# Third mixer: latents, keys and values copied in another order, transposes of the exponents two heads behind the scores, with a third buffer

## The chip, the core and the metric

The kernel runs on one core of a Trainium2 chip. A core has five engines that run their own instruction queues side by side and meet at semaphores: TensorE (PE in the rows; the loads of its weights are PEld), VectorE (DVE), ScalarE (ACT), GpSimd (POOL) and SyncE (SP), which here only issues DMAs. The metric is the device time of one execution in microseconds (us), and the figure given for a kernel is the median of its runs.

## The reference, cut to what matters

Two residual blocks work on 256 tokens of width 1024. The part that is changed is the last of three mixers, attention with latents:

```python
def mla_mixer(h, positions, w_in, q_norm_g, w_uq, kv_norm_g, w_ukv, w_o):
    q_a, kv_a, k_rope = jnp.split(h @ w_in, [Q_LORA, Q_LORA + KV_LORA], axis=-1)
    q = (rmsnorm_2(q_a, q_norm_g) @ w_uq).reshape(bsz, L, MLA_HEADS, QK_NOPE + QK_ROPE)
    q_nope, q_rope = q[..., :QK_NOPE], q[..., QK_NOPE:]
    kv = (rmsnorm_2(kv_a, kv_norm_g) @ w_ukv).reshape(bsz, L, MLA_HEADS, QK_NOPE + V_DIM)
    k_nope, v = kv[..., :QK_NOPE], kv[..., QK_NOPE:]
    q_rope = apply_rope(q_rope, cos[:, :, None], sin[:, :, None])
    k_rope = apply_rope(k_rope, cos, sin)
    ...
        s = (jnp.einsum("bqhd,bkhd->bhqk", qn, k_nope, preferred_element_type=jnp.float32)
             + jnp.einsum("bqhd,bkd->bhqk", qr, k_rope, preferred_element_type=jnp.float32)) * scale
        s = jnp.where(k_idx[None, :] <= q_idx[:, None], s, -jnp.inf)
        p = jax.nn.softmax(s, axis=-1).astype(v.dtype)
        return jnp.einsum("bhqk,bkhd->bqhd", p, v)
    ...
    return o @ w_o
```

There are 16 heads; the query latents have width 768, the latents of keys and values 256; a head has 64 unrotated and 32 rotated query and key rows and 64 value columns.

## The kernel before

All weights are streamed in blocks of 128x2048 numbers (1 MB). SP loads a block into one of three slots of `raw`. ACT rounds it to `whi` (`act_split`, line 176), DVE takes the residue `raw - whi` to `wlo` (`dve_split`, line 184), and PE multiplies in three passes: high by high, high by low and low by high. So each engine has splits standing in its queue among its other work, and their place in the queue is written out by hand. ACT may split a block once PE has used the block three before it; SP may load once DVE has split the block three before.

A block of the third mixer is numbered from `F0`: four blocks of the input projection, one of keys (`UKV0`, function `uk`), one of values (`uv`), eight of queries (`UQ0`, `uq`), four of the output projection (`OUT0`).

The entry of the mixer runs so. ACT copies each pair of latent tiles out of its bank (line 1785) and squares it (1787). PE sums the squares, ACT takes the root (`root`, 1773), DVE the reciprocal and the scaling by two multiplications per instruction (`scale_latent`, 1879 and 1882; group 0 are the two tiles for keys and values, group 1 the six for queries). ACT rounds a pair of scaled tiles to `xh` (`round_latent`, 1769), DVE takes the residue to `xl` (`rest`, 1870). PE computes keys for all heads into the four banks `ACC` (line 1628), the values into the banks `GATE`, `UP`, `MODP` and `STAT` (line 1646), and the first query block into `GATE` again (line 1670). The key copies of ACT (`m3_kt`, 1797), the value copies of ACT (1803) and of DVE (1908) empty these banks. The rotated part of the key is the same for all heads: `rotate_k` on DVE (lines 1890 to 1893) leaves it in `kr`, and GpSimd copies it 16 times into `m3_kt` (line 1849).

The attention then goes by turns `j`, each with one query block (two heads) and the scores of the two heads `h = 2 (j - 2)` and `h + 1`. A turn has on PE: half of the query block, `attend(h)`, the other half, `attend(h + 1)`, and `swap_q` (1681), which permutes rows for the rotation. For `swap_q` ACT first copies the query block to `m3_qs` (1841). GpSimd and DVE do the rotation: GpSimd multiplies by the cosine (1857), DVE by the sine (`rope_q`, 1917), GpSimd adds (1861). `attend(h)` has the scores into bank `h % 2` (1695, 1696 and the mask, 689), DVE's maxima (1923) and their scaling (1925), ACT's exponents (1811), DVE's reciprocals and weights (1929, 1932), the transposes of the exponents on PE into bank 2 (`turn`, 1705), ACT's copy to `m3_pt` (1818), for two heads the sums over the values into bank 3 (`sums`, 1716), and their split into `m3_o_hi` (ACT, 1828) and `m3_o_lo` (DVE, 1946). The exponents have two buffers, so that those of head `h` wait for the transposes of head `h - 2`. In the last turns the output projection (288) takes the place of the query blocks.

In the rows of the profile the tensors `m3_...` are called `m_...`, all PSUM banks `bank`, and `ident` is `consts`.

## Time and profile before

| | us |
|---|---|
| median of three runs | 1700.56 (1700.59, 1700.56, 1698.80) |
| the profiled execution | 1694.85 |
| its span, first to last instruction | 1693.2 |
| PE busy | 1659.2 (98%) |
| DVE busy | 1201.0 (71%) |
| ACT busy | 809.7 (48%) |
| POOL busy | 85.3 (5%) |
| mean granted TensorE clock | 0.992 of 2.4 GHz |

Busy time on an engine is no more than presence: PE is the engine on which nearly the whole chain of work lies that ended last (87% of it). The timeline lists instructions with start, length and, in brackets, how long the engine had been idle before and what released it. The third mixer fills the time from about 1353 to 1494 us.

### The profile page before, as it was taken

To read this page: it belongs to the slowest core of one execution; us is meant where nothing else is said; L and a number is where in the kernel's file an instruction comes from. 1 tells how busy PE (TensorE), PEld (TensorE's weight loads), DVE (VectorE), ACT (ScalarE), POOL (GpSimd) and SP (SyncE) were. 2 spreads that over 40 slices of the span, in tenths; PEclk is the share of its full clock that TensorE was granted. 3 is DMA by queue.
4 is the path that set the end of the run, shared out by engine and by line. 5 is a ranking of instruction groups with operands and counts; after the bars stand their busy time and mean duration, and the time that the engine had idled before them with its cause. 6 is when DMAs were issued, how large, how long until landed. Compare 5 with 4: busy or idle time off the path is not lost.

```text
span 1693.2 us, 34456 instructions
## 1 busy us (share of the span) xinstructions
PE 1659.2 (98%) x14544; PEld 1623.7 (96%) x14544; DVE 1201.0 (71%) x1303; ACT 809.7 (48%) x874; POOL 85.3 (5%) x110
## 2 busy tenths in 40 slices
PE   9999999999999999999998899999999999999998
PEld 9999999999999999999998899999999987899998
DVE  6888876676788886888867688756544566765444
ACT  5444556644544444444565554345344456554442
POOL 0000000000000000000003000000000003200000
PEclk9999999999999999999999999999999999999999
DMA  8998744344499874988533359653655433345551
GB/s 322 348 339 305 267 176 175 139 159 151 164 350 328 309 266 171 349 311 323 205 135 123 125 208 339 250 196 127 222 199 183 170 144 126 125 148 201 199 188 61
DMA packets 50491, 365.08 MB, mean 216 GB/s; under 512 B 5728, under 2 KB 5856, under 8 KB 6240
## 3 DMA queue, kind: packets, MB, share of 16 engines
q1 hardware_dynamic: 39744, 287.04, 46.2%
q0 software_dynamic: 10368, 75.50, 12.0%
q8 instruction: 74, 1.21, 0.3%
q10 hardware_dynamic: 288, 1.18, 0.2%
q14 instruction: 17, 0.14, 0.0%
HBM read 362.65 MB, written 1.05 MB: 215 GB/s over the span
## 4 chain that ended last, share of the span: by engine, by line
PE 87%; DVE 7%; ACT 3%; issue 1%; DMA 1%; SPq 0%; ACTq 0%; DVEq 0%
PE bank L252 50%; PE bank L288 24%; PE bank L271 3%; PE bank L244 3%; DVE wlo L184 2%; PE bank L361 2%; PE bank L1670 1%; PE bank L373 1%; ACT whi L176 1%; DVE m_p L1435 1%; DVE m_e L1932 0%; DVE x L313 0%; ACT m_e L1811 0%; DMA raw<-stream_in 0%; DVE x L405 0%
## 5 line engine op out<-in xcount | busy, mean ns | idle before, releaser
L184 DVE TENSOR_TENSOR wlo<-raw,whi 128x2048 fp32r<-128x2048 f32 x261 | 598.1, 2294 | 200.7 <-ACT whi L176 200.2
L252 PE MATMUL bank<-xh,whi 128*128 128x256 f32 x2608 | 727.3, 279 | 3.5 <-DVE wlo L184 1.9
L252 PE MATMUL bank<-xl,whi 128*128 128x256 f32 x2608 | 721.7, 277 | 0.0
L252 PE MATMUL bank<-xh,wlo 128*128 128x256 f32 x2608 | 721.4, 277 | 0.0
L176 ACT ACTIVATE whi<-raw 128x2048 fp32r<-128x2048 f32 x261 | 498.2, 1913 | 300.4 <-PE bank L252 177.1
L252 PEld LDWEIGHTS bank<-xh,whi 128*128 128x128 f32 x2608 | 491.1, 188 | 6.1 <-issue 3.2
L252 PEld LDWEIGHTS bank<-xl,whi 128*128 128x128 f32 x2608 | 490.1, 188 | 0.1
L252 PEld LDWEIGHTS bank<-xh,wlo 128*128 128x128 f32 x2608 | 490.0, 188 | 0.0
L288 PE MATMUL bank<-hid_hi,whi 128*128 128x256 f32 x1056 | 291.9, 276 | 0.0
L288 PE MATMUL bank<-hid_lo,whi 128*128 128x256 f32 x1056 | 291.5, 276 | 0.0
L288 PE MATMUL bank<-hid_hi,wlo 128*128 128x256 f32 x1056 | 291.5, 276 | 0.0
L288 PEld LDWEIGHTS bank<-hid_hi,whi 128*128 128x128 f32 x1056 | 198.2, 188 | 0.4
L288 PEld LDWEIGHTS bank<-hid_lo,whi 128*128 128x128 f32 x1056 | 198.2, 188 | 0.0
L288 PEld LDWEIGHTS bank<-hid_hi,wlo 128*128 128x128 f32 x1056 | 198.2, 188 | 0.0
L541 ACT ACTIVATE hid_hi<-hid 128x512 fp32r<-128x512 f32 x66 | 41.8, 633 | 281.9 <-DVE hid L570 281.9
L585 DVE SCALAR_TENSOR_TENSOR mod_acc<-mod_raw,c_act,mod_acc 128x1024 f32<-128x1024 f32 x126 | 161.5, 1282 | 2.6
L570 DVE TENSOR_TENSOR hid<-gate,bank 128x512 f32<-128x512 f32 x66 | 45.3, 686 | 77.7 <-PE bank L252 77.5
L2005 POOL DMA_DIRECT2D mod_raw<-mod_in x72 | 38.3, 533 | 931.0 <-DVE mod_acc L585 919.2
L572 DVE TENSOR_TENSOR hid_lo<-hid,hid_hi 128x512 fp32r<-128x512 f32 x66 | 45.8, 693 | 46.2 <-ACT hid_hi L541 46.2
L361 PE MATMUL bank<-ident_b 128*128 128x128 bf16 x690 | 50.1, 231 | 0.0
L361 PEld LDWEIGHTS bank<-ident_b 128*128 128x128 bf16 x690 | 47.0, 108 | 0.2
L666 DVE SCALAR_TENSOR_TENSOR m_pre<-bank,params,m_pre 128x255 f32<-128x255 f32 (+2 forms) x84 | 34.0, 473 | 14.8 <-ACT m_pre L653 14.8
(317 smaller groups left out, 1819.6 us busy)
## 6 DMA issues: line engine op xcount, KB each, us to landing
raw<-stream_in SPq DMA_DIRECT2D x270, 1024.0 KB, 4.8
mod_raw<-mod_in POOLq DMA_DIRECT2D x72, 1024.0 KB, 7.3
params<-params_in SPq DMA_DIRECT2D x1, 1474.0 KB, 16.0
x<-x_in SPq DMA_DIRECT2D x2, 512.0 KB, 4.5
m_gsu<-sgu_in ACTq DMA_DIRECT2D x1, 1024.0 KB, 5.1
y_out<-x SPq DMA_DIRECT2D x1, 1024.0 KB, 3.8
consts<-consts_in SPq DMA_DIRECT2D x1, 280.5 KB, 4.8
tab_pos<-pos_in ACTq DMA_DIRECT2D x1, 128.0 KB, 3.3
```

Source lines behind the costliest of these rows:

```text
L176: act.activation(whi[:, s, :], raw[:, s, :], ACT.Copy).then_inc(sem("w_hi_ready"), 1)
L184: dve.tensor_tensor(wlo[:, s, :], raw[:, s, :], whi[:, s, :].bitcast(F32), ALU.subtract)\
L244: last = pe.matmul(out[:, m, :], w[:, s, c:c + P], (xh, xl)[part][:, k, :], start=(part == 0 and k == 0 and m == 0 and w is whi), stop=(pa ...
L252: last = pe.matmul(out[:, m, :], (whi, wlo)[wp][:, s, k * 256 + m * P:k * 256 + m * P + P], (xh, xl)[ap][:, k, :], start=(k == 0 and j == ...
L271: last = pe.matmul(out[:, tt, :], (xh, xl)[ap][:, k, tt * P:tt * P + P], (whi, wlo)[wp][:, s, k * 256:k * 256 + 256], start=(k == 0 and j ...
L288: mm = pe.matmul(pair(acc[d // 2])[:, d % 2, :], (whi, wlo)[wp][:, s, c:c + P], (hi, lo)[ap][:, kt, :], start=(first and d % 2 == 0 and kt ...
L361: pe.matmul(bank_[:, 0:P], ident_b[:, :], ident_b[:, :], start=True, stop=True, skip_group_check=True)
L541: act.activation(hid_hi[:, parity], hid[:, :, :], ACT.Copy).then_inc(sem("hid_rounded"), 1)
L570: dve.tensor_tensor(hid[:, :, :], gate[:, :, :], pair(UP), ALU.mult).then_inc(sem("hid_ready"), 1)
L572: dve.tensor_tensor(hid_lo[:, parity], hid[:, :, :], hid_hi[:, parity].bitcast(F32), ALU.subtract)\
L585: ins = dve.scalar_tensor_tensor(out=mod_acc[:, :], in0=mod_raw[:, s, t * D:t * D + D], scalar=c_act[:, k:k + 1], in1=mod_acc[:, :], op0=A ...
L2005: pool.dma_start(mod_raw[:, s, :], a_mod[ds(s * P + 2 * P * turn, P), :])\
```

## The change

Six things are done, all in the third mixer.

1. On DVE the residue of the key and value latents (`rest(3)`) stands ahead of the split of block F0 + 5 instead of behind it.
2. On GpSimd the copy of the rotated key waits also until ACT has squared the last pair of latents.
3. On ACT the three roundings of the query latents stand ahead of the key copies, instead of between them; the first copy of values and the split of block F0 + 7 stand ahead of the key copies, the second copy of values behind them. The value copies wait for their own bank (`m3_v_bank`) instead of for the whole block.
4. On DVE the first value copy waits for its own bank, and the second stands behind the split of F0 + 7.
5. The transposes of head `h` come with `attend(h + 2)` instead of `attend(h + 1)`; those of heads 14 and 15 both with `attend(16)`. With them go ACT's copies. The exponents have a third buffer, in `rows`.
6. The sums of heads 2k and 2k + 1, with their high and low parts, come with `attend(2k + 4)` instead of `attend(2k + 3)`; the last stay with `attend(17)`.

On ACT, entry of the mixer, from the second root to the first copy of `m_qs`. Before:

```order
L1773 ACTIVATE m_e<-bank,cols 128x256
L1797 ACTIVATE m_kt<-bank 64x2x256 x2
L1769 ACTIVATE xh<-xm 128x512
L1797 ACTIVATE m_kt<-bank 64x2x256 x2
L1769 ACTIVATE xh<-xm 128x512
L1797 ACTIVATE m_kt<-bank 64x2x256 x2
L1769 ACTIVATE xh<-xm 128x512
L1797 ACTIVATE m_kt<-bank 64x2x256 x2
L1803 ACTIVATE m_v<-bank 128x512 x2
L176 ACTIVATE whi<-raw 128x2048 x2
L1841 ACTIVATE m_qs<-bank 96x512
```

After:

```order
L1784 ACTIVATE m_e<-bank,cols 128x256
L1780 ACTIVATE xh<-xm 128x512 x3
L1808 ACTIVATE m_v<-bank 128x512
L176 ACTIVATE whi<-raw 128x2048
L1813 ACTIVATE m_kt<-bank 64x2x256 x8
L1816 ACTIVATE m_v<-bank 128x512
L176 ACTIVATE whi<-raw 128x2048
L1853 ACTIVATE m_qs<-bank 96x512
```

The roundings, one value copy and one split have moved ahead of all eight key copies; the number of instructions up to `m_qs` is the same.

On DVE, the same stretch, from the scaling of the key and value latents on. Before:

```order
L1882 SCALAR_TENSOR_TENSOR xm<-xm,params,m_e 128x256 x2
L184 TENSOR_TENSOR wlo<-raw,whi 128x2048
L1870 TENSOR_TENSOR xl<-xm,xh 128x512
L184 TENSOR_TENSOR wlo<-raw,whi 128x2048
L1879 RECIPROCAL m_e<-m_e 128x256
L1882 SCALAR_TENSOR_TENSOR xm<-xm,params,m_e 128x256 x6
```

After:

```order
L1895 SCALAR_TENSOR_TENSOR xm<-xm,params,m_e 128x256 x2
L1883 TENSOR_TENSOR xl<-xm,xh 128x512
L184 TENSOR_TENSOR wlo<-raw,whi 128x2048 x2
L1892 RECIPROCAL m_e<-m_e 128x256
L1895 SCALAR_TENSOR_TENSOR xm<-xm,params,m_e 128x256 x6
```

The residue has changed places with the first of the two splits.

On ACT, one turn of the attention, from the exponents of an even head to those of the odd one and what follows. Before:

```order
L1811 ACTIVATE m_e,m_nm<-bank,m_nm 128x256
L1818 ACTIVATE m_pt<-bank 128x384
L176 ACTIVATE whi<-raw 128x2048
L1841 ACTIVATE m_qs<-bank 96x512
L1811 ACTIVATE m_e,m_nm<-bank,m_nm 128x128
L1811 ACTIVATE m_e,m_nm<-bank,m_nm 128x256
L1818 ACTIVATE m_pt<-bank 128x384
L1828 ACTIVATE m_o_hi<-bank 128x256
```

After:

```order
L1823 ACTIVATE m_e,m_nm<-bank,m_nm 128x256
L1830 ACTIVATE m_pt<-bank 128x384
L1840 ACTIVATE m_o_hi<-bank 128x256
L176 ACTIVATE whi<-raw 128x2048
L1853 ACTIVATE m_qs<-bank 96x512
```

The copy of the sums, `m_o_hi`, has moved from the end of the turn to a place ahead of the split and of `m_qs`.

The diff, cut to its core:

```diff
+        probs = (e3[:, 0, :], e3[:, 1, :], rows[:, 0:2, :].rearrange("p a t -> p (a t)")[:, 0:384])
+        def turned_at(h):
+            return tuple(t for t in ((h - 2, h - 1) if h == MLA_H else (h - 2,)) if 0 <= t < MLA_H and (t < MLA_H - 1 or h == MLA_H))
+        def summed_at(h):
+            if h == MLA_H + 1:
+                return MLA_H // 2 - 1
+            return (h - 4) // 2 if h >= 4 and h % 2 == 0 else None
...
             def attend(h):
                 if 0 <= h < MLA_H:
                     scores(h)
-                if 1 <= h <= MLA_H:
-                    turn(h - 1)
-                if 3 <= h < MLA_H + 2 and h % 2 == 1:
-                    sums((h - 3) // 2)
+                for t in turned_at(h):
+                    turn(t)
+                if summed_at(h) is not None:
+                    sums(summed_at(h))
...
             act_split(act, F0 + 6)
             root(1)
+            for b in range(3):
+                round_latent(b)
+            act.wait_ge(sem("m3_v_bank"), 1)
+            act.activation(v3[:, 0, 0:512], V_BANKS[0][:, :], ACT.Copy).then_inc(sem("m3_v_act"), 1)
+            act_split(act, F0 + 7)
             act.wait_ge(sem("w_used"), F0 + UKV0 + 1)
             for q in range(4):
                 for r in range(2):
                     act.activation(kt[0:64, 4 * q + r:4 * q + r + 3:2, :], pair(ACC[q])[64 * r:64 * r + 64], ACT.Copy)\
                        .then_inc(sem("m3_k"), 1)
-                if q < 3:
-                    round_latent(q)
-            act.wait_ge(sem("w_used"), F0 + UKV0 + 2)
-            for i in range(2):
-                act.activation(v3[:, i, 0:512], V_BANKS[2 * i][:, :], ACT.Copy).then_inc(sem("m3_v_act"), 1)
-            act_split(act, F0 + 7)
+            act.wait_ge(sem("m3_v_bank"), 3)
+            act.activation(v3[:, 1, 0:512], V_BANKS[2][:, :], ACT.Copy).then_inc(sem("m3_v_act"), 1)
 
             def exps(h):
                 act.wait_ge(sem("m3_max"), h + 1)
-                if h >= 2:
-                    act.wait_ge(sem("m3_turned"), h - 1)
+                if h >= 3:
+                    act.wait_ge(sem("m3_turned"), h - 2)
...
             pool.wait_ge(sem("m3_kr"), 3)
+            pool.wait_ge(sem("m3_squared"), 4)
             pool.tensor_copy(kt[64:DQ, :, :], kr[64:DQ, :].unsqueeze(1).to_broadcast([32, MLA_H, T]))\
...
             scale_latent(0)
+            rest(3)
             dve_split(dve, F0 + 5)
-            rest(3)
             dve_split(dve, F0 + 6)
             scale_latent(1)
             for b in range(3):
                 rest(b)
-            for i in range(2):
-                dve.wait_ge(sem("w_used"), F0 + UKV0 + 2)
-                dve.tensor_copy(v3[:, i, 512:D], V_BANKS[2 * i + 1][:, :]).then_inc(sem("m3_v_dve"), 1)
+            dve.wait_ge(sem("m3_v_bank"), 2)
+            dve.tensor_copy(v3[:, 0, 512:D], V_BANKS[1][:, :]).then_inc(sem("m3_v_dve"), 1)
             dve_split(dve, F0 + 7)
+            dve.wait_ge(sem("w_used"), F0 + UKV0 + 2)
+            dve.tensor_copy(v3[:, 1, 512:D], V_BANKS[3][:, :]).then_inc(sem("m3_v_dve"), 1)
```

`attend` on ACT and DVE follows `turned_at` and `summed_at` in the same way, and `e3[:, h % 2, ...]` becomes `probs[h % 3][...]` in the transposes, exponents and weights.

## Rows read from the trace of the kernel before

**Rows 1.** Waits in 1355 to 1530 us: engine, line, releaser, total us, times, longest.
```profile
PE bank L1705 <- DVE m_e L1932: 1.0, 3, 0.4
```

**Rows 2.** Timeline of PE: start, length, instruction, idle before and its releaser.
```profile
1384.59 0.36 PE L1628 MATMUL bank<-xh,whi 128*128 128x256 f32 x1 [2.30 <-DVE xl L1870]
...
1400.21 0.33 PE L1670 MATMUL bank<-xh,whi 128*96 128x256 f32 x1 [1.79 <-ACT m_v L1803]
...
1405.30 0.67 PE L1681 MATMUL bank<-m_qs,consts 96*96 96x512 f32 x1 [0.68 <-ACT m_qs L1841]
```

**Rows 3.** Timeline of ACT at the entry of the mixer.
```profile
1382.32 0.63 ACT L1769 ACTIVATE xh<-xm 128x512 fp32r<-128x512 f32 x1 [3.17 <-PE bank L252]
...
1398.24 1.21 ACT L1797 ACTIVATE m_kt<-bank 64x512 f32<-64x512 f32 x2
...
1400.44 3.72 ACT L176 ACTIVATE whi<-raw 128x2048 fp32r<-128x2048 f32 x2
1404.65 0.59 ACT L1841 ACTIVATE m_qs<-bank 96x512 f32<-96x512 f32 x1 [0.48 <-PE bank L1670]
```

**Rows 4.** Timeline of DVE at the entry of the mixer.
```profile
1379.16 2.48 DVE L1882 SCALAR_TENSOR_TENSOR xm<-xm,params,m_e 128x256 f32<-128x256 f32 x2
...
1383.76 0.68 DVE L1870 TENSOR_TENSOR xl<-xm,xh 128x512 fp32r<-128x512 f32 x1
1385.94 2.29 DVE L184 TENSOR_TENSOR wlo<-raw,whi 128x2048 fp32r<-128x2048 f32 x1 [1.50 <-ACT whi L176]
1389.38 1.75 DVE L1879 RECIPROCAL m_e<-m_e 128x256 f32<-128x256 f32 x1 [1.15 <-ACT m_e L1773]
1391.16 2.47 DVE L1882 SCALAR_TENSOR_TENSOR xm<-xm,params,m_e 128x256 f32<-128x256 f32 x6
...
1402.39 4.49 DVE L184 TENSOR_TENSOR wlo<-raw,whi 128x2048 fp32r<-128x2048 f32 x2 [2.25 <-ACT whi L176]
```

**Rows 5.** Timeline of POOL at the entry of the mixer.
```profile
1377.35 3.61 POOL L1849 COPY m_kt<-rows 32x4096 f32<-32x4096 f32 x1 [311.88 <-DVE rows L1893]
1405.40 2.64 POOL L1857 TENSOR_TENSOR m_t<-m_qs,cos 96x512 f32<-96x512 f32 x1 [24.43 <-ACT m_qs L1841]
```

**Rows 6.** Timeline of PE, one turn of the attention.
```profile
1448.03 0.38 PE L1695 MATMUL bank<-m_kt,m_qt 96*128 96x128 f32 x2
...
1451.22 0.38 PE L1695 MATMUL bank<-m_kt,m_qt 96*128 96x128 f32 x2
...
1452.73 0.87 PE L1716 MATMUL bank<-m_pt,m_v 128*64 128x256 f32 x8
1453.53 1.10 PE L1681 MATMUL bank<-m_qs,consts 96*96 96x512 f32 x2
...
1456.58 0.39 PE L1695 MATMUL bank<-m_kt,m_qt 96*128 96x128 f32 x2
```

**Rows 7.** Timeline of ACT, the same turn.
```profile
1449.86 0.37 ACT L1811 ACTIVATE m_e<-bank,m_nm 128x128 f32<-128x128 f32 x1 [3.55 <-DVE m_nm L1925]
...
1452.84 0.59 ACT L1841 ACTIVATE m_qs<-bank 96x512 f32<-96x512 f32 x1
...
1454.48 0.39 ACT L1828 ACTIVATE m_o_hi<-bank 128x256 fp32r<-128x256 f32 x1
```

**Rows 8.** Timeline of DVE, the same turn and two turns on.
```profile
1449.02 0.60 DVE L1923 TENSOR_REDUCE m_nm<-bank 128x1 f32<-128x128 f32 x2
...
1465.18 0.83 DVE L1925 TENSOR_SCALAR m_nm<-m_nm 128x2 f32<-128x2 f32 x1
```

**Rows 9.** Timeline of POOL beside rows 8.
```profile
1453.51 1.27 POOL L1857 TENSOR_TENSOR m_t<-m_qs,cos 96x512 f32<-96x512 f32 x1 [1.72 <-ACT m_qs L1841]
...
1464.69 1.29 POOL L1861 TENSOR_TENSOR m_qt<-m_qt,m_t 96x512 f32<-96x512 f32 x1 [1.35 <-DVE m_qt L1917]
```

**Rows 10.** Busy us and (xcount) per engine in two stretches, PEclk, DMA share, GB/s.
```profile
931.00:936.00 5.00, 2.23 (x22) 1.51 (x21) 4.13 (x9) 1.70 (x6) 0.00 (x0) 0.96 0.57 206
936.00:938.00 2.00, 1.56 (x9) 0.85 (x9) 0.78 (x3) 0.83 (x2) 0.00 (x0) 0.50 0.02 8
```

More of the change, by code:

```diff
@@ L1704, in turn @@
                 for c in range(3):
-                    mm = pe.transpose(ACC[2][:, c * P:c * P + P], e3[:, h % 2, c * P:c * P + P], ident)
+                    mm = pe.transpose(ACC[2][:, c * P:c * P + P], probs[h % 3][:, c * P:c * P + P], ident)
                 mm.then_inc(sem("m3_turned"), 1)
@@ L1822, in attend @@
                     exps(h)
-                if 1 <= h <= MLA_H:
-                    turned(h - 1)
-                if h >= 3 and h % 2 == 1:
-                    k = (h - 3) // 2
+                for t in turned_at(h):
+                    turned(t)
+                if summed_at(h) is not None:
+                    k = summed_at(h)
                     act.wait_ge(sem("m3_sums"), 2 * k + 2)
@@ L1931, in weights @@
                 for lt, (c0, c1) in enumerate(((0, P), (P, 384))):
[L1932 removed]
+                    dve.tensor_scalar(probs[h % 3][:, c0:c1], probs[h % 3][:, c0:c1], nm[:, h, 6 + lt:7 + lt], None, ALU.mult)\
                        .then_inc(sem("m3_p"), 1)
@@ L1942, in attend @@
                     weights(h)
-                if h >= 3 and h % 2 == 1:
-                    k = (h - 3) // 2
+                if summed_at(h) is not None:
+                    k = summed_at(h)
                     dve.wait_ge(sem("m3_o_hi"), k + 1)
```

3 lines of the change are left out of this document (1 added, 2 removed).

## Prediction

> **What bounds the kernel now.** The page comes first: TensorE (PE) is busy nearly all the time, so what counts is the little time in which it waits, and what comes to stand in its way. The change touches the third mixer alone, so the next view is the list of who waited for whom in that stretch, where PE's waits for the exponents' transposes are short, 1.0 us over three [rows 1], and then the timeline, engine by engine. On PE there are two long waits: 2.30 us ahead of the keys' matmuls (L1628), ended by the residue of the latents on DVE, and 1.79 us ahead of the first query block (L1670), ended by ACT's copy of the values; a shorter one of 0.68 us stands ahead of the first swap (L1681) [rows 2]. ACT copies keys, latents and values without a break to 1400.44 and then splits two blocks before it copies m_qs for that swap [rows 3]. In the attention, a turn of two heads repeats every 8.55 us (1448.03 to 1456.58) [rows 6]. There PE hardly waits, but DVE and ACT stand in the same ring: scores, maxima, exponents, transposes' copy, weight split, m_qs, swap, next scores [rows 6 to 8]. Swap starts 0.69 us after m_qs has started, and a m_qs copy followed by a waiting swap takes 0.65 us [rows 2, 3, 6, 7]: the ring has no more than 0.05 us of slack.
>
> **Part 1, the latents' residue ahead of a split.** Today rest(3) comes at 1383.76 behind a split, and PE starts 0.83 us later, at 1384.59 [rows 2, 4]. Moved ahead, it waits for ACT's rounding only, which begins at 1382.32 and takes 0.63 us [rows 3]: it starts at 1382.97. **Minus 0.8 us**, and PE starts at 1383.8. PE then has unbroken work up to 1398.42 (the wait of 1.79 us counted back from 1400.21), now up to 1397.6.
>
> **Part 2, the copy of the rotated key on GpSimd.** It takes 3.61 us and starts at 1377.35 [rows 5]. While it runs, two of DVE's multiplications of 128x256 take 2.48 us; six take 2.47 us when it doesn't [rows 4]. So one engine is shut out until the other's instruction ends. The reverse is there too: a rotation of GpSimd that takes 1.27 us elsewhere (the row at 1453.51) takes 2.64 us from 1405.40, while DVE's splits last to about 1406.8 [rows 4, 5, 9]. The new wait (m3_squared at 4) lets the copy go when ACT has squared the last latents. ACT's next split ends at 1385.94 [rows 4], and takes about 1.9 us (3.72 us for two [rows 3]), so that is 1384.0. By then DVE has been in the moved split since 1383.6 (rest(3) and 0.6 us). That ends at 1385.8; the next split must wait for ACT until 1385.94. In this gap of 0.14 us, an estimate from these rows, the waiting copy takes its turn and holds it to about 1389.4. The split then ends at 1391.6 instead of 1388.2; the reciprocal (1.75 us) and six multiplications (2.47 us) of the query latents end at 1395.8, where they now end at 1393.6 and would end at 1392.8 with part 1 alone.
> The Trainium skill (SBUF — State Buffer, "Who interferes with whom") calls this pair of ports an exclusive lock, held for a whole instruction, rather than a division of bandwidth. By a division, DVE would lose only part of the 3.61 us and the entry below would come out nearer to rival 1; the row of 2.48 us speaks for the lock.
>
> **Part 3, the new order on ACT.** Last rounding at 1395.8, 0.5 us; values 0.5 us; split 1.8 us; eight key copies at 0.61 us (two take 1.21 us [rows 3]), 4.9 us; values 0.5 us (about 1 us for two, from the last key copies to 1400.44); split 1.8 us: m_qs starts at 1405.85 and PE's swap 0.65 us later, at 1406.5. Today the swap is at 1405.30 [rows 2]. The first query block itself starts early, at about 1397.9, since its bank is free and its residues are ready; the 1.79 us of wait go. But that gives nothing: PE then stands from 1402.1 to 1406.5, where it waited 0.68 us. What was a wait ahead of L1670 is now a longer one ahead of L1681. **Entry: plus 1.2 us.**
>
> **Part 4, the clock.** A pause of 4.4 us is nearly twice the longest of this stretch today, 2.30 us [rows 2]. The one stretch like it is that of 931 to 936 us: PE busy for 2.23 of 5 us, then the clock at 0.50 (1.2 instead of 2.4 GHz), also in 936 to 938 [rows 10]. Behind the pause PE works without a break for its own query block, so half speed costs half of the slow time. Between none and some 6 us of slow clock, an estimate from the length of that block (4 us and the swap): 0 to 3 us. I take **plus 1.5 us**, the middle.
> The Trainium skill (TensorE: Matmul & The Clock Gate, "What's actually happening") has the idle array fall back to 1.2 GHz and rise only after sustained work. By that rule alone a loss would be near certain and I would take the upper half, 2 to 3 us.
>
> **Part 5, the transposes two heads back.** The transposes then find their exponents ready; PE's short wait ahead of every second one goes. It is worth 0.3 us a turn at most (1.0 us over three [rows 1]), and only if PE sets the pace, yet the ring above does. And the sums of a pair move from the odd head to the even one, and with them ACT's copy m_o_hi (0.39 us, of which I take 0.1 to overlap the next instruction) from behind the exponents of the odd head [rows 7] to ahead of the split, inside the ring: swap moves by 0.3 less the slack, **0.25 us for each of the four turns** that have both sums and a query block (heads 4 to 11). On PE the sums (0.80 us from 1452.73 to 1453.53) now stand ahead of the odd head's scores, which start 3.99 us after the even head's instead of 3.19. Maxima 0.99 us later, exponents (0.84 us on), weights, the split and the next maxima: this second ring is about 0.1 us a turn longer still. Four turns: 1.0 to 1.4 us. DVE's o_lo moves along, ahead of the odd head's maxima, where DVE waits for PE anyway. The third buffer costs nothing: same sizes, same engines.
> The exit has one more: turns 14 and 15 share bank 2 and now follow each other, with ACT's copy between them, about as long as one m_qs copy with a waiting swap, 0.65 us, against some 0.4 us of wait saved at the old turn(14). **Attention in all: plus 1.3 us.**
>
> **Part 6, a close race.** The scaling of the maxima (L1925) takes 0.17 us and 0.83 us at 1465.18, shut out by a GpSimd rotation that had begun at 1464.69 [rows 8, 9]. Today the odd head's scaling is over well before the next rotation: scores at 1451.22, rotation at 1453.51 [rows 6, 9]. After the change the odd scores are 0.8 us later or a little more and the rotation 0.3 us: scaling starts at 1451.22 + 0.8 + 0.99 + 0.6 = 1453.6, and each tenth that PE loses around the sums closes the gap; rotation at 1453.8. If the rotation wins, ACT's exponents wait up to 1.1 us more and the turn is that much longer; the next turn is then out of the race. Two turns are at risk: 0 to 2.2 us; I take **0.5 us**.
>
> **Sum.** 1.2 + 1.5 + 1.3 + 0.5 = 4.5 us. The profiled execution took 1694.85 us (span 1693.2); so it would take 1699.4. The median of the runs shown is 1700.56, so 1705.0. Own range of this case: 1.2 + 0 + 1.0 + 0 to 1.2 + 2.5 + 1.4 + 1.1 (one lost race), that is 1702.8 to 1706.8.
>
> **Rivals.** *1, the copy on GpSimd harms nobody*: DVE keeps its turn across the gap of 0.14 us, or the copy is slowed instead. Then the latents are ready at 1392.8 to 1394, ACT reaches m_qs 1.8 to 2.8 us earlier than above, the swap moves by -0.6 to -1.5 us, the pause is 2 to 3 us and the clock holds; with the attention's 1.3 us the sum is about 0: 1700.5. Against it: both shut-outs in [rows 4, 5]; for it: the gap is small.
> *2, PE sets the pace (faster)*: ACT is idle for 3.55 us of each turn [rows 7]; if its copy hides there and the roundings and copies pack tighter than 0.6 us, the swaps come as soon as PE is ready. Gain: 0.8 at the keys, up to 1.79 + 0.68 at the query block, 0.3 in six turns: 2.5 to 5 us, 1696.5. It decides if m_qs starts before 1402. Against it: the idle 3.55 us lie ahead of the exponents, not between them and m_qs.
> *3, clock and race both go wrong*: slow clock from 1406 on for nearly 7 us (3.4 us), both races lost: 1.2 + 3.4 + 1.5 + 2.2 = 8.3, 1709. For it: the scaling at 1465.18 did lose [rows 8, 9]; against it: at 1453 it wins with room.
>
> **How the numbers follow.** A difference below 0.2% (3.4 us) can't be told from none in this kernel. The forecast case has 0.55, of which 0.42 above 1703.96 and 0.13 below it; rival 1 0.20, no change; rival 2 0.13, of which 0.10 faster by over 0.2%; rival 3 0.12, slower. So faster 0.10, same 0.36, slower 0.54. The range leaves out most of rival 2 and the far end of rival 3: 1699.0 to 1709.0.
>
> **What would show it.** Right: a DVE split of over 5 us next to a GpSimd copy from 1384 on; PE idle for about 4 us ahead of the first swap, none ahead of L1670; a granted clock below 1.00 from 1404 to 1412; turns of 8.8 us or more for heads 4 to 11, with PE waiting at L1681. Wrong: a split of 2.3 us there (part 2 falls, and 4 with it); turns of 8.3 us (part 5); no scaling of 0.8 us or longer among the odd heads (part 6).

## The result and the profile after

| | median of the runs | runs | lowest to highest | profiled execution | its span |
|---|---|---|---|---|---|
| before | 1699.31 us | 11 | 1694.25 to 1701.9 | 1694.85 us | 1693.2 |
| after | 1705.84 us | 11 | 1701.37 to 1709.67 | 1702.05 us | 1700.4 |

The ratio of after to before is 1.0038, with a 95% interval of 1.0024 to 1.0051: slower by 4.1 to 8.7 us. The forecast was 1705.0, slower. The number holds, but it was put together wrongly in four places (the clock, the turns, the exit and the race), as the sections below show. Two disturbed executions, one of sums_exit_behind (2363 us) and one of the kernel before beside it (4244 us), are left out of the ratios further down.

Line numbers move between the kernels: the first swap is L1681 before and L1692 after, m_qs L1841 and L1853, the keys L1628 and L1639, the query blocks L1670 and L1681, the scaling of the maxima L1925 and L1939, its rotation on GpSimd L1857 and L1870, the transposes L1705 and L1716, the sums L1716 and L1727. In the experiments they move by a few lines more.

Because single executions of one kernel differ by several microseconds elsewhere, times inside the third mixer are compared as **distances** from one event that all kernels share, DVE's first multiplication in the rotation of the key part. In the timelines of DVE, before and then after:

```profile
1376.07 0.42 DVE L1890 TENSOR_TENSOR m_t<-m_qs,cos 96x256 f32<-96x256 f32 x1 [0.77 <-PE bank L1604]
```
```profile
1375.72 0.42 DVE L1903 TENSOR_TENSOR m_t<-m_qs,cos 96x256 f32<-96x256 f32 x1 [0.77 <-PE bank L1615]
```

The other end is the sums of the last pair, before and after, in PE's timeline (start, length, instruction, idle before):

```profile
1477.55 0.52 PE L1705 MATMUL bank<-consts,m_e 128*128 128x128 f32 x3 [0.45 <-DVE m_e L1932]
...
1484.90 0.87 PE L1716 MATMUL bank<-m_pt,m_v 128*64 128x256 f32 x8
```
```profile
1487.77 0.55 PE L1716 MATMUL bank<-consts,m_e 128*128 128x128 f32 x3 [0.58 <-ACT m_pt L1830]
...
1491.97 0.87 PE L1727 MATMUL bank<-m_pt,m_v 128*64 128x256 f32 x8
```

1484.90 − 1376.07 = 108.83 us before, 1491.97 − 1375.72 = 116.25 after: 7.4 us more, all of it inside this mixer. The two profiled executions differ by 7.2 us as a whole. The medians differ by 6.5, with an interval that holds both figures.

**The entry, after.** On PE the pause ahead of the keys is 1.54 us where it was 2.30 [rows 2], the 1.79 us ahead of the first query block are gone, and the first swap waits 4.41 us where it waited 0.68:

```profile
1383.47 0.36 PE L1639 MATMUL bank<-xh,whi 128*128 128x256 f32 x1 [1.54 <-DVE xl L1883]
...
1406.01 1.17 PE L1692 MATMUL bank<-m_qs,consts 96*96 96x512 f32 x1 [4.41 <-ACT m_qs L1853]
```

DVE and GpSimd, to be read beside [rows 4, 5]:

```profile
1382.63 0.69 DVE L1883 TENSOR_TENSOR xl<-xm,xh 128x512 fp32r<-128x512 f32 x1 [2.94 <-ACT xh L1780]
1383.24 7.89 DVE L184 TENSOR_TENSOR wlo<-raw,whi 128x2048 fp32r<-128x2048 f32 x2
1391.06 1.74 DVE L1892 RECIPROCAL m_e<-m_e 128x256 f32<-128x256 f32 x1
1392.83 2.47 DVE L1895 SCALAR_TENSOR_TENSOR xm<-xm,params,m_e 128x256 f32<-128x256 f32 x6
```
```profile
1383.88 5.11 POOL L1862 COPY m_kt<-rows 32x4096 f32<-32x4096 f32 x1 [320.04 <-ACT m_v L1798]
```

Two splits take 7.89 us, of which the second alone has 5.55, from 1385.59. The copy is shown as under way at 1383.88, while the first split runs, and takes 5.11 us instead of 3.61 [rows 5]: 1.5 us in which it waits for the port, up to about the end of the first split, and then its own 3.61 while the second split stands. ACT's rounding that the second split needs ended at 1385.55 and the first split at about the same time, so the gap in which the copy came in was under 0.1 us. DVE's latents are ready at 1392.83 + 2.47 = 1395.3. From there ACT runs without a break to m_qs; note its order, roundings, value, split, keys:

```profile
1395.87 0.58 ACT L1808 ACTIVATE m_v<-bank 128x512 f32<-128x512 f32 x1
1396.35 1.90 ACT L176 ACTIVATE whi<-raw 128x2048 fp32r<-128x2048 f32 x1
1398.15 4.91 ACT L1813 ACTIVATE m_kt<-bank 64x512 f32<-64x512 f32 x8
1403.09 0.60 ACT L1816 ACTIVATE m_v<-bank 128x512 f32<-128x512 f32 x1
1403.58 1.90 ACT L176 ACTIVATE whi<-raw 128x2048 fp32r<-128x2048 f32 x1
1405.38 0.58 ACT L1853 ACTIVATE m_qs<-bank 96x512 f32<-96x512 f32 x1
```

**The clock, after.** Stretches of 2 us; the columns are the stretch, its length, busy us (and count) of PE, weight loads, DVE, ACT and GpSimd, then TensorE's clock, the DMA share and GB/s. The clock goes to its lower level (0.50 is 1.2 of 2.4 GHz) in the pause, at about 1404.5, and stays there for about 5 us of full work:

```profile
1404.00:1406.00 2.00, 0.00 (x0) 0.00 (x0) 0.49 (x1) 2.00 (x3) 0.00 (x0) 0.61 0.45 188
1406.00:1408.00 2.00, 1.99 (x3) 0.85 (x4) 1.81 (x1) 1.76 (x1) 1.89 (x1) 0.50 0.00 0
1408.00:1410.00 2.00, 2.00 (x12) 2.00 (x11) 1.93 (x2) 0.00 (x0) 1.86 (x2) 0.50 0.44 90
1410.00:1412.00 2.00, 2.00 (x14) 2.00 (x14) 1.09 (x1) 0.00 (x0) 2.00 (x1) 0.69 1.01 426
1412.00:1414.00 2.00, 1.70 (x16) 1.48 (x14) 0.00 (x0) 0.26 (x1) 0.24 (x1) 1.00 0.78 246
```

**The attention, after.** Two of the four turns of heads 4 to 11 are 9.9 us long, the other two 8.7 and 8.8; before, all were 8.56. In each long one the scaling of the odd head's maxima, 0.17 us of work, takes 1.22 us. GpSimd's rotation had begun 0.08 us earlier (POOL, DVE, then ACT, whose exponents wait for the scaling):

```profile
1439.74 1.27 POOL L1870 TENSOR_TENSOR m_t<-m_qs,cos 96x512 f32<-96x512 f32 x1 [1.98 <-ACT m_qs L1853]
```
```profile
1439.16 0.62 DVE L1937 TENSOR_REDUCE m_nm<-bank 128x1 f32<-128x128 f32 x2 [0.72 <-PE bank L689]
1439.82 1.22 DVE L1939 TENSOR_SCALAR m_nm<-m_nm 128x2 f32<-128x2 f32 x1
...
1458.50 1.22 DVE L1939 TENSOR_SCALAR m_nm<-m_nm 128x2 f32<-128x2 f32 x1
```
```profile
1441.07 0.37 ACT L1823 ACTIVATE rows<-bank,m_nm 128x128 f32<-128x128 f32 x1 [1.41 <-DVE m_nm L1939]
```

The list of waits of 1355 to 1530 us has PE waiting 10.7 us for m_qs in 8 turns; its entry for the exponents ahead of the transposes, 1.0 us before [rows 1], is gone:

```profile
PE bank L1692 <- ACT m_qs L1853: 10.7, 8, 4.4
```

For heads 4 to 11 PE's timeline gives the waits as 0.26, 1.40, 0.26 and 1.39 us, 3.31 in all. In the kernel before it waits 0.18 us in these four turns. The rest of the time is the same, 34.0 and 34.1 us: before, TensorE had practically no time to spare there, and what the turns grew by is waiting for m_qs.

### The profile page after: what moved, and what is told of

The parts are those of the page before. It is cut to its first block, busy times and chain, and to the rows that moved or that the text cites. A ratio compares the mean times of both kernels' runs of the same rounds, so it can differ in the third digit from the quotient of the medians.

```text
span 1700.4 us, 34456 instructions
## 1 busy us (share of the span) xinstructions
PE 1659.7 (98%) x14544; PEld 1624.0 (96%) x14544; DVE 1205.1 (71%) x1303; ACT 810.1 (48%) x874; POOL 86.8 (5%) x110
## 3 DMA queue, kind: packets, MB, share of 16 engines
HBM read 362.65 MB, written 1.05 MB: 214 GB/s over the span
## 4 chain that ended last, share of the span: by engine, by line
PE 89%; DVE 6%; ACT 4%; issue 1%; DMA 0%; SPq 0%; ACTq 0%; DVEq 0%
PE bank L252 50%; PE bank L288 24%; PE bank L244 3%; PE bank L271 3%; PE bank L361 2%; DVE wlo L184 2%; ACT whi L176 1%; PE bank L1681 1%; PE bank L373 1%; DVE m_p L1435 1%; PE bank L1692 0%; DVE x L313 0%; DVE x L405 0%; PE bank L1171 0%; PE bank L740 0%
```

## The experiments

Each kernel is told as a change to the changed kernel unless it says otherwise. This table gives distances in us, read from the timelines. The keys' first matmul, the first swap and the last sums are counted from the multiplication named above, the other columns are times between two events. "heads 4 to 11" is the time from the fourth to the eighth and last swap (`swap_q(3)` to `swap_q(7)`), four turns.

| kernel | keys | first swap | first to second swap | heads 4 to 11 | last swap to last sums | last sums |
|---|---|---|---|---|---|---|
| before | 8.52 | 29.23 | 5.86 | 34.26 | 22.80 | 108.83 |
| after | 7.75 | 30.29 | 8.37 | 37.31 | 23.65 | 116.25 |
| copy_at_once | 7.95 | 27.83 | 5.93 | 37.30 | 23.56 | 111.25 |
| entry_alone | 7.75 | 30.30 | 8.38 | 34.25 | 22.71 | 112.32 |
| attention_alone | 8.52 | 30.94 | 5.98 | 37.31 | 23.55 | 114.40 |
| attention_again | 8.52 | 29.42 | 5.97 | 36.23 | 24.77 | 113.01 |
| before_again | 8.52 | 31.01 | 5.98 | 34.26 | 22.79 | 110.70 |
| warm | 7.95 | 30.49 | 5.87 | 37.30 | 23.55 | 113.84 |
| rotation_behind | 7.74 | 30.28 | 8.44 | 35.31 | 23.56 | 114.22 |
| high_rotation_behind | 7.75 | 30.29 | 7.52 | 35.40 | 23.61 | 113.45 |
| entry_best | 7.94 | 26.70 | 5.97 | 34.24 | 22.81 | 106.39 |
| entry_and_race | 7.75 | 26.68 | 5.93 | 35.23 | 23.57 | 107.96 |
| sums_behind | 7.75 | 26.51 | 5.97 | 34.20 | 24.25 | 107.55 |
| sums_exit_behind | 7.74 | 26.66 | 5.97 | 34.13 | 25.27 | 108.65 |

And the whole kernel against before in the same comparison, where it was timed:

| kernel | median us | before | ratio, 95% interval |
|---|---|---|---|
| copy_at_once | 1700.91 | 1699.23 | 1.0010, 0.9994 to 1.0025 |
| entry_alone | 1701.02 | 1699.23 | 1.0016, 1.0003 to 1.0029 |
| attention_alone | 1701.19 | 1699.23 | 1.0019, 1.0006 to 1.0031 |
| warm | 1702.17 | 1699.23 | 1.0020, 1.0005 to 1.0035 |
| rotation_behind | 1703.13 | 1698.69 | 1.0019, 1.0006 to 1.0033 |
| high_rotation_behind | 1702.95 | 1698.69 | 1.0030, 1.0017 to 1.0044 |
| entry_best | 1694.54 | 1698.69 | 0.9971, 0.9958 to 0.9984 |
| entry_and_race | 1698.31 | 1698.69 | 0.9993, 0.9982 to 1.0004 |
| sums_behind | 1697.22 | 1698.14 | 0.9989, 0.9976 to 1.0003 |
| sums_exit_behind | 1697.80 | 1698.14 | 0.9992, 0.9978 to 1.0006 |

The ratio is estimated from the runs themselves and is not the quotient of the two medians. An interval is some 4 us wide, so these order the large steps only; a step of 1 us is read from the first table, which has one profiled execution per kernel.

### The copy on GpSimd

```diff
             pool.wait_ge(sem("m3_kr"), 3)
-            pool.wait_ge(sem("m3_squared"), 4)
             pool.tensor_copy(kt[64:DQ, :, :], kr[64:DQ, :].unsqueeze(1).to_broadcast([32, MLA_H, T]))\
```

> The changed kernel without the new wait of GpSimd's copy of the rotated key (it starts again as soon as the key is rotated). Distances are counted from the first multiplication of rotate_k on DVE; in the kernel before the first swap stands at 29.2 us, in the changed one at 30.3, and the last sums at 108.8 and 116.3. My theory (the copy takes the port in the gap between two splits and delays the query latents by 3.3 us, which makes PE stand for 4.4 us and then run at 1.2 GHz): the two splits take 2.3 us each, the first swap comes at 27.7, PE stands about 2 us ahead of it, the granted clock stays at 1.00, last sums at about 111; the median 5 us below the changed kernel's, 1.5 to 2.5 us above the one before. Rival (the new order of the copies on ACT is what delays the swap and lowers the clock): first swap at 29.5 or later, clock at 0.50 for some us, the median within 2 us of the changed kernel's.

The first swap came at 27.83 and the last sums at 111.25, 5.0 us less than in the changed kernel. One wait decides both the entry and the clock. POOL, then DVE:

```profile
1379.69 3.60 POOL L1861 COPY m_kt<-rows 32x4096 f32<-32x4096 f32 x1 [312.76 <-DVE rows L1905]
```
```profile
1381.50 2.46 DVE L1894 SCALAR_TENSOR_TENSOR xm<-xm,params,m_e 128x256 f32<-128x256 f32 x2
...
1386.13 4.64 DVE L184 TENSOR_TENSOR wlo<-raw,whi 128x2048 fp32r<-128x2048 f32 x2
...
1392.91 2.47 DVE L1894 SCALAR_TENSOR_TENSOR xm<-xm,params,m_e 128x256 f32<-128x256 f32 x6
```

The copy shuts out the two multiplications again, as before, and the splits take 4.64 us, 3.25 less than with the copy behind them. PE's pause ahead of the swap is 1.83 us, and the clock holds. So what the new wait saves, 1.6 us on the multiplications, it loses twice over on the splits. The rival, the new order of ACT's copies, falls: that order is still there.

### Entry and attention apart

entry_alone is the changed entry with the attention of the kernel before; attention_alone the entry of before with the changed attention. The core of entry_alone, beside the buffers and waits that go with it:

```diff
-            return tuple(t for t in ((h - 2, h - 1) if h == MLA_H else (h - 2,)) if 0 <= t < MLA_H and (t < MLA_H - 1 or h == MLA_H))
+            return (h - 1,) if 1 <= h <= MLA_H else ()
...
-            if h == MLA_H + 1:
-                return MLA_H // 2 - 1
-            return (h - 4) // 2 if h >= 4 and h % 2 == 0 else None
+            return (h - 3) // 2 if 3 <= h < MLA_H + 2 and h % 2 == 1 else None
```

> The changed entry of the mixer (parts 1 to 4 of the change, with the new wait of GpSimd's copy), with the attention of the kernel before. My theory, in which entry and attention add up: first swap at 30.3 us, second at 38 to 39 (35.1 in the kernel before) if the clock falls, last sums at 112.4, the median 3.5 us above the one before. Rival (the attention's new order costs nothing, all lies in the entry): last sums at 115 to 116, the median 6.5 us above.

> The changed attention (transposes two heads behind, third buffer, sums at the even head) behind the entry of the kernel before. My theory: first swap at 29.2 us, clock at 1.00, the four turns of heads 4 to 11 take 8.8 to 9.9 us each instead of 8.56, in two of them the scaling of the maxima takes 1.2 us; last sums at 112.7, the median 3.9 us above the one before. Rival (the attention suffers only because it starts behind a late entry): turns of 8.5 us or less, the median within 1 us of the one before.

entry_alone: last sums at 112.32, which is 3.49 more than before, 1.07 of it at the first swap and 2.52 at the second; its rival falls. attention_alone: the turns were as expected, which disposes of its rival, but the first swap was 1.7 us late, which the expectation doesn't explain. Its windows show the clock at 0.50 behind the pause of 2.30 us ahead of the keys, a pause that the kernel before has too:

```profile
1392.00:1394.00 2.00, 1.55 (x12) 1.58 (x13) 0.51 (x2) 1.76 (x1) 0.00 (x0) 0.96 0.39 119
1394.00:1396.00 2.00, 2.00 (x6) 1.64 (x6) 2.00 (x1) 0.00 (x0) 0.00 (x0) 0.50 0.97 406
1396.00:1398.00 2.00, 2.00 (x8) 1.63 (x8) 0.08 (x1) 0.00 (x0) 0.00 (x0) 0.69 0.34 61
```

So this kernel and the kernel before were profiled a second time, unchanged.

> The kernel of attention_alone a second time, for one question: in its profile the clock was at 0.50 from 1394 to 1396 us, behind the pause of 2.30 us ahead of the keys' matmuls, which the kernel before also has, at full clock. Theory (that fall is by the execution, not by the kernel): the clock stays at 1.00 there, the first swap stands 29.2 us behind the first multiplication and not 30.9, and the last sums at 112.7. Rival (the kernel's own timing brings it about): 0.50 again, 30.9 and 114.4.

> The kernel before a second time, for the same question. Theory (the fall behind the pause of 2.30 us comes in some executions of any kernel that has the pause): either outcome is open in a single look; the first swap stands at 29.2 us with the clock at 1.00, or at 30.9 with a stretch at 0.50. Rival (only attention_alone has it): 29.2.

This time attention_again kept the full clock (swap at 29.42, last sums at 113.01, 0.3 more than expected), and it was the kernel before that lost it, with the first swap at 31.01:

```profile
1384.00:1386.00 2.00, 0.98 (x6) 1.01 (x7) 0.87 (x2) 2.00 (x2) 0.00 (x0) 0.87 0.38 49
1386.00:1388.00 2.00, 2.00 (x10) 1.91 (x9) 1.64 (x1) 0.33 (x1) 0.00 (x0) 0.50 0.88 369
1388.00:1390.00 2.00, 2.00 (x8) 1.69 (x8) 0.66 (x1) 0.00 (x0) 0.00 (x0) 0.77 0.54 139
```

The rival of both expectations falls: the same code with the same pause of 2.30 us runs on at 2.4 GHz in one execution and falls to 1.2 GHz in another, two of four profiles, at 1.5 to 1.8 us a time. None of the ten profiles with the changed residue and its pause of 1.5 us showed it there. The Trainium skill (TensorE: Matmul & The Clock Gate, "What's actually happening") says that the window over which the hardware watches the array runs freely and doesn't start with the kernel, and that the number of slow matmuls at a kernel's start varies from run to run for that reason. These two pairs agree as far as the varying goes; no run here shows the reason.

Without this stray 1.5 us, attention_again against before gives 4.2 us for the attention, and entry_alone 3.5 for the entry. Together 7.7, where the whole change shows 7.4: by the distances the two halves add up. The medians can't confirm it: they were expected 3.5 and 3.9 us above before and came 1.8 and 2.0 above, with intervals of 0.5 to 4.9 and 1.0 to 5.3 us.

In attention_again the second lost race (the races have their own section below) came one turn later than in the others, behind the last swap (the turns are 36.23, the stretch behind them 24.77). The sum of both columns is the same as in attention_alone to 0.2 us.

### The clock

```diff
             def swap_q(j):
+                if j == 0:
+                    pe.wait_ge(sem("m3_v_dve"), 2)
+                    for _ in range(64):
+                        pe.matmul(STAT[:, 0:P], ident_b[:, :], ident_b[:, :], start=True, stop=True, skip_group_check=True)
```

> The changed kernel with 64 idle matmuls of 128x128 in bf16 on PE, written to the free bank STAT while PE waits for the first swap; nothing else is changed. My theory (of the 3.6 us that the second swap is late, 2.5 us are half clock after the pause): the granted clock stays at 1.00 from 1400 to 1415, the first swap stays at 30.3 us, the second comes at 36.2 instead of 38.7, the median 2.5 us below the changed kernel's. Rival (the late second swap has another cause, a wait for the weights or for ACT): second swap at 38 or later in spite of the full clock.

64 matmuls into a bank that nobody reads, ahead of the first swap: with them in the pause the clock stays at 1.00, the first swap is no earlier (30.49) and the second is 5.87 us behind it instead of 8.37. The rival falls. The clock alone costs 2.5 us: half of the 5 us or so in the windows above.

### The lost races

```diff
                 pool.wait_ge(sem("m3_qs"), j + 1)
+                if j >= LAG:
+                    pool.wait_ge(sem("m3_max"), 2 * (j - LAG) + 2)
```

> The changed kernel with one more wait: from the third query block on, GpSimd starts its cosine rotation only when the maxima of the odd head whose scores stand beside it are taken and scaled. So the scaling (0.17 us) cannot be shut out by the rotation (1.27 us) any more; the entry is unchanged. Theory (two lost races cost the changed kernel about 1.35 us each): no scaling of 0.8 us or longer is left in the turns that have a query block, the four turns of heads 4 to 11 take 8.6 to 8.9 us each where they took 8.71, 9.91, 8.77 and 9.92, and the last sums start 113.6 us after the first multiplication of the rotation, 2.7 less than in the changed kernel. Rival (the length of these turns comes from the place of the sums and of ACT's copies, and a won race only moves the wait): at least two turns still take 9.5 us or more and the last sums stay at 115.5 us or later. A second rival: the rotation that now starts later delays the split block and the swap: all four turns at 9.2 us, the last sums at 115.

Both rivals fall. The turns are 8.76, 8.89, 8.77 and 8.89 us, and the four together 2.0 us shorter (35.31 against 37.31). Here is the place where the race was lost, POOL and DVE:

```profile
1441.79 1.27 POOL L1872 TENSOR_TENSOR m_t<-m_qs,cos 96x512 f32<-96x512 f32 x1 [2.36 <-DVE m_nm L1941]
```
```profile
1440.83 0.62 DVE L1939 TENSOR_REDUCE m_nm<-bank 128x1 f32<-128x128 f32 x2 [0.72 <-PE bank L689]
1441.48 0.17 DVE L1941 TENSOR_SCALAR m_nm<-m_nm 128x2 f32<-128x2 f32 x1
```

A race costs 1.0 us, not the 1.35 of the expectation: 1.05 us of the scaling, while the longer turn of 8.9 us is there with the race won. The last sums came 0.6 us later than expected, about the 2 times 0.35 by which the races were overpriced.

### Where the rest of the turn comes from

high_rotation_behind puts ACT's copy of the sums, and DVE's residue, back to the end of the turn:

```diff
-                if summed_at(h) is not None:
...
+                if summed_at(h) is not None and not (h % 2 == 0 and 4 <= h < 12):
+                    high(summed_at(h))
+
+            def high(k):
+                act.wait_ge(sem("m3_sums"), 2 * k + 2)
+                act.activation(o_hi[:, k, :], ACC[3][:, 0:T], ACT.Copy).then_inc(sem("m3_o_hi"), 1)
...
                 if h >= 0:
                     attend(h + 1)
+                if h % 2 == 0 and 4 <= h < 12:
+                    high(summed_at(h))
...
```

> As rotation_behind, and besides, in heads 4 to 11, ACT's copy of the sums (m_o_hi) and DVE's residue of them (o_lo) go back from the head of the turn to its end, behind the copy of m_qs; the sums on TensorE stay ahead of the odd head's scores. This takes the copy of 0.39 us out of the ring that sets the swap. Theory of the prediction (the copy is worth 0.25 us a turn, the place of the sums 0.1 us): the four turns come to 8.6 us each, the last sums at about 1 us less than in rotation_behind. Rival (the place of the sums ahead of the odd scores carries the longer turn, ACT's copy hides): the turns stay within 0.1 us of those of rotation_behind and the last sums within 0.4 us.

The rival is right: 35.40 us against 35.31. The last sums were 0.8 us earlier, but all of that, 0.9 us, lies between the first swap and the second, where no sums are yet: in this execution the clock fell only 0.7 us behind the first swap (0.91 in 1409.0 to 1409.5) instead of in the pause, and was low for 3.4 us instead of 5. The turns alternate now, 8.44, 9.23, 8.56 and 9.17, but the pairs are as long as in rotation_behind. PE, one pair of scores and swaps:

```profile
1445.47 0.87 PE L1727 MATMUL bank<-m_pt,m_v 128*64 128x256 f32 x8
...
1448.40 0.38 PE L1706 MATMUL bank<-m_kt,m_qt 96*128 96x128 f32 x2
...
1450.53 1.10 PE L1692 MATMUL bank<-m_qs,consts 96*96 96x512 f32 x2 [0.87 <-ACT m_qs L1855]
```

The sums still stand 3 us ahead of the odd scores, and the wait has only moved. sums_behind therefore puts the sums themselves back, on all engines, behind the odd scores and ahead of that head's transposes, with the good entry and the won races of entry_and_race (below):

```diff
-            if h == MLA_H + 1:
-                return MLA_H // 2 - 1
-            return (h - 4) // 2 if h >= 4 and h % 2 == 0 else None
+            if h >= MLA_H:
+                return h - MLA_H + 6 if h < MLA_H + 2 else None
+            return (h - 5) // 2 if h >= 5 and h % 2 == 1 else None
...
                     scores(h)
+                if summed_at(h) is not None and h < MLA_H:
+                    sums(summed_at(h))
                 for t in turned_at(h):
                     turn(t)
-                if summed_at(h) is not None:
+                if summed_at(h) is not None and h >= MLA_H:
```

> As entry_and_race (good entry, transposes two heads behind with the third buffer, no lost races), with one thing more undone: in the heads with scores, the sums of a pair, ACT's copy of them and DVE's residue stand again with the odd head, behind its scores, as in the kernel before. Theory (the place of the sums, 0.8 us of TensorE between the even and the odd scores, is what makes the changed turns 8.76 and 8.9 us long, not the transposes two heads back): the turns are 8.56 us again or up to 0.3 shorter, the last but one swap 75.1 us or less after the first multiplication, where entry_and_race had 75.57, and 83.6 or less at the last, where it had 84.39. Rival (the transposes two heads behind cost by themselves, as ACT's copy of them no longer waits and moves in the ring): turns of 8.75 us or more.

The turns are 8.50, 8.57, 8.57 and 8.56: as before, with the transposes still two heads back and the third buffer still there. PE:

```profile
1450.68 0.39 PE L1706 MATMUL bank<-m_kt,m_qt 96*128 96x128 f32 x2
...
1451.54 0.87 PE L1727 MATMUL bank<-m_pt,m_v 128*64 128x256 f32 x8
1452.34 0.55 PE L1716 MATMUL bank<-consts,m_e 128*128 128x128 f32 x3
1453.04 1.10 PE L1692 MATMUL bank<-m_qs,consts 96*96 96x512 f32 x2
```

So the place of the sums makes the turn 0.26 us longer (35.23 in entry_and_race against 34.20), and the transposes two heads back neither cost nor give anything in the turns. The longer turn is again waiting: with the sums ahead of the odd scores and the races won (rotation_behind) PE waits 1.28 us for m_qs in the four turns, and with them behind 0.39.

### The exit

> As sums_behind, and the transposes of head 14 go back to head 15, so that the turns of 14 and 15 don't follow each other through the one bank. Theory of the prediction (the exit costs 0.25 us for that reason): from the last swap to the last sums it is 23.0 us or less, where the changed kernel and entry_and_race have 23.6 and the kernel before 22.8. Rival (the exit is longer because more sums and transposes are left for its end): still 23.4 us or more.

As a change to sums_behind:

```diff
-            return tuple(t for t in ((h - 2, h - 1) if h == MLA_H else (h - 2,)) if 0 <= t < MLA_H and (t < MLA_H - 1 or h == MLA_H))
+            back = {MLA_H - 1: (h - 2, h - 1), MLA_H: (h - 1,)}.get(h, (h - 2,) if h < MLA_H else ())
+            return tuple(t for t in back if t >= 0)
```

My theory falls and the rival stands: 25.27 us, a microsecond more than sums_behind. The transposes of head 14 now follow those of 13 through the one bank, and ACT's copy between them stands behind a split and the exponents of head 15:

```profile
1478.44 0.55 PE L1717 MATMUL bank<-consts,m_e 128*128 128x128 f32 x3
1480.58 0.55 PE L1717 MATMUL bank<-consts,rows 128*128 128x128 f32 x3 [1.59 <-ACT m_pt L1833]
```

Counting PE's rows behind the last swap explains nearly all of it. Before, that stretch holds five heads' transposes and two pairs' sums ahead of the last; in the changed kernel, sums_behind and sums_exit_behind it holds six and three. The extra pieces take 0.45 us (from the start of the transposes at 1477.55 to the next instruction at 1478.00) and 0.80 us, as [rows 6] has for the sums. That is 1.25; with the waits' differences (0.58 or 1.59 against 0.45, and a wait of 0.42 against 0.32 ahead of the first output block) it gives 24.3 and 25.3 us for sums_behind and sums_exit_behind, which took 24.25 and 25.27. For the changed kernel, which has no wait of 0.32 there, it gives 23.9, and 23.65 was measured; where the 0.2 us are is open. And the two turns ahead of head 4, from which that work was taken, got only 0.05 us shorter (16.63 against 16.68): PE waits longer for m_qs there instead, 1.28 and 0.99 us in the changed kernel against 0.38 and none before. So in those turns TensorE waits in place of the work, and the work came to stand where TensorE sets the pace.

### Two kernels put together from this

entry_best has the attention of the kernel before; entry_and_race the changed attention and the wait of rotation_behind. Both have this entry:

```diff
             for j in range(M3_TURNS):
                 h = 2 * (j - LAG)
                 attend(h)
-                act_split(act, F0 + UQ0 + j + 2)
+                if j > 0:
+                    act_split(act, F0 + UQ0 + j + 2)
...
+                if j == 0:
+                    act_split(act, F0 + UQ0 + 2)
...
             pool.wait_ge(sem("m3_kr"), 3)
-            pool.wait_ge(sem("m3_squared"), 4)
+            pool.wait_ge(sem("m3_split"), 4)
```

> The attention of the kernel before, and an entry with the two parts of the change that give something, and without the two that cost: latents' residue ahead of a split as in the change; GpSimd's copy of the rotated key waits until DVE has begun the splits' last block ahead of the reciprocal (a wait on the split counter at 4), where it stands beside work that doesn't share the port; the values' copies in the changed order; ACT copies the first m_qs ahead of its second split. Theory (the first swap is set by ACT's row of copies and by what the copy on GpSimd takes from DVE): first swap 26.4 us after the first multiplication of the rotation (29.2 before, 30.3 after), no DVE split of over 4 us, a clock of 1.00 throughout, the last sums at 106 us (108.8 before), the whole 2.8 us shorter than before, 1696.5 beside 1699.2. Rival (what is won at the entry is lost again in the attention, because its ring starts in another phase): first swap as said, last sums at 108 us or later, no difference in the whole.

> The entry of entry_best with the attention of the changed kernel and the wait of rotation_behind. Theory (entry, clock and lost races are all that is wrong with the changed kernel, but for 0.1 to 0.35 us a turn of the ring): first swap at 26.4 us, no slow clock, turns of 8.6 to 8.9 us, the last sums at 107.2 us, 1.6 us less than before and 9 us less than in the changed kernel; the whole about 1697.7 beside 1699.2. Rival (the attention two heads back has a loss of its own that grows when TensorE is never late): the last sums at 109 us or later.

The copy now runs at 1399.81, beside a copy on DVE out of a bank, which it doesn't slow (0.69 us), and m_qs goes ahead of a split. But the expectation that no DVE split takes over 4 us is wrong: the split of F0 + 7, ready 1.2 us after the copy had begun, takes 4.56 us instead of 2.3 (4.37 to 4.56 in the four kernels with this entry). It costs nothing here because no wait of TensorE up to the first swap hangs on it. POOL, DVE and PE of entry_best:

```profile
1399.81 3.61 POOL L1863 COPY m_kt<-rows 32x4096 f32<-32x4096 f32 x1 [329.15 <-DVE xl L1884]
```
```profile
1388.59 4.64 DVE L184 TENSOR_TENSOR wlo<-raw,whi 128x2048 fp32r<-128x2048 f32 x2
...
1399.94 0.69 DVE L1921 COPY m_v<-bank 128x512 f32<-128x512 f32 x1 [0.27 <-PE bank L1655]
1401.01 4.56 DVE L184 TENSOR_TENSOR wlo<-raw,whi 128x2048 fp32r<-128x2048 f32 x1 [0.37 <-ACT whi L176]
```
```profile
1407.58 1.10 PE L1690 MATMUL bank<-m_qs,consts 96*96 96x512 f32 x2 [0.68 <-ACT m_qs L1852]
```

The first swap came at 26.70, and the gain of 2.4 us stays to the last sums: the rival (lost again in the attention) falls. The median is 4.2 us below before, the ratio's interval ends at 0.9984: it is faster than before by a little, and so than the changed kernel. That the median gains more than the distance may be chance, or come from the fall of the clock behind the keys' pause, which before has in some executions and this kernel had not in its profile; how often it comes was not counted. entry_and_race has the same swap and 1.6 us more at the last sums (107.96, expected 107.2; its rival, 109 or later, falls): that is the changed attention, races won. As a whole it can't be told from the kernel before (interval up to 1.0004).

## Why the prediction was right, and where it was not

The 7.42 us by place, from the first table: 1.06 at the first swap, 2.51 up to the second, −0.05 in two turns, 3.05 in the four turns of heads 4 to 11, 0.85 behind the last swap.

- **Part 1, the residue** (−0.8 us at the keys): right, 8.52 to 7.75 us.
- **Part 2, the GpSimd copy**: right, to the step: it took its turn between two splits, the splits took 3.25 us more (3.4 in the sum), and copy_at_once removes it. The gap was under 0.1 us and not 0.14; whether the copy needs a gap at all was not tested. The latents were ready at 1395.3, forecast 1395.8. Rival 1 falls. The rule of the port as an exclusive lock in the Trainium skill (SBUF — State Buffer, "Who interferes with whom") agrees: 5.11 us for a copy of 3.61 beside 7.89 for splits of 4.64.
- **Part 3, the entry** (+1.2): 1.06, pause 4.41 as forecast (4.4). Rival 2 needed m_qs ahead of 1402 and it came at 1405.38.
- **Part 4, the clock** (+1.5, from 0 to 3): right in kind, a term sized too low. warm gives 2.5; in high_rotation_behind nearly the same pause (4.31) cost 1.65, so the price differs between executions. "I take the middle" was a choice without a row: the one comparable stretch [rows 10] fell, and by the Trainium skill's rule (TensorE: Matmul & The Clock Gate, "What's actually happening"), which the prediction cites, it would have been 2 to 3.
- **Part 5, the turns** (+1.0 for four): measured 1.05 with the races won, but for another reason, so that the fit of this number is luck. The step "ACT's copy of the sums is in the ring and costs 0.25 us a turn" is false: moved back it gives nothing (35.40 against 35.31). The step "sums ahead of the odd scores, 0.1 us" is the true one, and is worth 0.26. With the sums back behind the odd scores, the turns are 8.50 to 8.57 again.
- **Part 5, the exit** (+0.25): measured 0.85. The step that failed looked only at two turns that share a bank, and left out that one head's transposes and one pair's sums had moved behind the last swap, 1.25 us of work. "Shared bank, 0.25 us" was tested by sums_exit_behind, which got longer.
- **Part 6, the race** (0.5): both races lost, 2.0 us. The working itself gave 1453.6 against 1453.8 and named every tenth as a threat; with 0.2 us between two events that are forecast to no better than 0.5, the middle of 0 to 2.2 was the value to take, at least.

So the mechanism is nearer to rival 3 (clock and race both wrong), which had 0.12, than to the forecast's own sum of 4.5. That the median fell on the forecast all the same is luck in the baseline. The three runs that were shown had a median of 1700.56, the eleven 1699.31: with the right terms, 1700.56 + 7.4 = 1708.0 would have been forecast, and 1705.84 measured. And the medians differ by 6.5, not 7.4, which the interval of 4.1 to 8.7 us doesn't tell apart; the fall of the clock that the kernel before has in some executions would work that way, but this is argued, not shown. The sign, the direction of every term and the range of 1699.0 to 1709.0 were right; the forecast case's own range, 2.2 to 6.2 us more, was too low for the 7.4 of the trace, and the sum was 2.9 us too small.

## What to carry to other kernels

A GpSimd copy that waited here for the port had it before DVE's next split, and the two splits took 3.25 us more: place such a copy, by a semaphore, where the instructions that it shuts out are on no path to TensorE, not at the earliest moment. Look at what really stands beside it: in entry_best it still shut out a split, at no cost. Moving work back by a head or two isn't free even where nothing waits for it: count what then stands behind the last step that other work covers, and count what it pushes in front of. Where two events are forecast within a few tenths of each other, the forecast can't say which comes first: price the bad outcome at half or more.

## What the hardware showed that was not expected

- A DVE instruction of 0.17 us with an operand of 128x2 took 1.22 to 1.27 us behind a rotation on GpSimd that had begun 0.02 to 0.08 us before it, twice in each profile of a kernel with the changed attention and without the added wait (five profiles).
- The same kernel with the same pause of 2.30 us on TensorE kept 2.4 GHz in one execution and fell to 1.2 GHz in another, at 1.5 to 1.8 us; pauses of 4.3 to 4.4 us fell each time (four profiles), and 64 small matmuls in such a pause prevented it.
- The price of that pause is not fixed: from the first swap to the second it was 8.37 to 8.44 us in three kernels and 7.52 in a fourth with the same entry (high_rotation_behind), against 5.87 at the full clock. In the fourth the clock fell 0.7 us behind the pause instead of in it.
- A DVE split that became ready while GpSimd's copy of 3.61 us was under way took 4.37 to 4.56 us instead of 2.3 (four kernels), while a DVE copy of 128x512 out of a bank, beside the same copy, took its usual 0.69 us.
